# Chunk 0's own convolution taps in a bank of their own, and chunk 7's diagonals built earlier

## The chip, the cores and the metric

One NeuronCore of one Trainium2 chip runs the whole program. The metric is the device time of one execution in microseconds (us), the median of the runs.

## The reference, cut to what matters

The program computes two transformer-like layers (a pooling mixer, sliding-window attention, two gated feed-forward blocks), and after them a block with a Conformer convolution and an MLP, all in float32 for 512 tokens of width 1024. The change lies within the Conformer convolution:

```python
def conformer_conv(x, w_in, b_in, conv_w, conv_b, ln_g, ln_b, w_out, b_out):
    a, g = jnp.split(x @ w_in + b_in, 2, axis=-1)
    h = a * jax.nn.sigmoid(g)
    h = lax.conv_general_dilated(          # depthwise, 31 taps, padded in front
        h, conv_w[:, None, :].astype(h.dtype), window_strides=(1,),
        padding=[(CONV_KERNEL - 1, 0)],
        dimension_numbers=("NWC", "WIO", "NWC"),
        feature_group_count=D_MODEL) + conv_b
    h = jax.nn.silu(layer_norm(h, ln_g, ln_b))
    return h @ w_out + b_out
```

Each of the 1024 channels is convolved with 31 taps of its own: the output at token t is the sum over k of w[k] times h[t - 30 + k], plus a bias.

## The kernel before, in words

Activations lie transposed: 128 channels on the partitions and 512 tokens along them, so the 1024 channels are 8 chunks (C = 8). Five engines work side by side: TensorE (PE), VectorE (DVE), ScalarE (ACT), GpSimd (POOL) and SyncE (SP, which issues DMAs). Each runs its own list of instructions in order and waits for the others by semaphores.

**Projections.** A weight unit is 128 columns of a weight matrix. SP loads it into one of four slots of `raw` (L460), ACT makes the rounded high part `whi` (L988), and the low part `wlo` = raw - whi is made by DVE (`split_lo`, L1349), or, for the fourteen units of `OTHER_LOW` (6 to 19), by POOL (L602) or by an adding DMA that POOL issues (L596) after ACT has negated the high part (L1270). A chain is 8 tiles of three matmuls each (L628 to L630), 24 in all, into one of the banks 0 to 3. Units 0 to 15 of the stage `ain` are the gate and the value halves of the 8 chunks in turn: chains 2c and 2c+1 belong to chunk c.

**The convolution of chunk c.** DVE evicts the gate half (`evict(c, 0)`, L1750) to `tmp`, ACT takes its sigmoid (L1283), DVE evicts the value half to `taps`, which is bank 5 (`evict(c, 1)`, L1750), and forms hc (L1760) from `taps` and the sigmoid. The 31 taps of hc are then shared out:

- PE takes `PE_TAPS[c]` of them as matmuls with diagonal matrices (`convolve`, L906). For these, SP issues `SHIFTS[c]` DMAs (`shift_hc`, L496) that copy hc into `shifted` at several offsets, and DVE builds the diagonals `dg` in one instruction (`diagonals`, L1728). They sum in bank 6 or 7 (by c mod 2).
- ACT multiplies `POOL_TAPS[c]` of them (L1261) into a ring of nine buffers `tapped`, and POOL adds these up in `prod` (L614). ACT waits for POOL to give back a buffer of the ring.
- DVE takes the rest: its own taps (`own_tap`, L1704 for the first and L1707 for the others), done before PE's matmuls on the same bank, and `LATE_TAPS[c]` late ones (L1717), done after them and during the next chunk. Chunk 0 has 12 own taps and 2 late ones, chunk 1 seven and 8, chunk 6 three and none, chunk 7 eleven and none.

At the end `collect(c)` (L1744) adds bank 6 or 7 and `prod` into `hv`. ACT squares `hv` (L1278), and PE sums both over the channels (`statistics`, L920).

**Which comes first in a bank.** For the chunks 0 to 6 DVE's first own tap writes bank 6 or 7 and PE's diagonal matmuls add to it, so `convolve(c)` waits until all own taps are done (L902). Chunk 7 (`APART`) is treated otherwise: its own taps go to `taps` and the last of them to `hv`, PE's first round opens the bank with `start`, and `collect` first adds `prod` and `hv` (L1739) and then the bank. Ahead of the stage, in `first_chains`, PE writes banks 6 and 7 once with a matmul each (L656).

**The order of the work.** PE (L924 to L935): in the round of chunk c the two chains of chunk c, `convolve(c - 1)`, `statistics(c - 3)`. Chunk 0's two chains are interleaved, with the feature sums of the norm (L672) ahead of their last tiles; DVE makes the norm's `rinv` from these (L1771 to L1776) before the first eviction. DVE (L1764 to L1803): in the round of c, `gated(c)` (value eviction and hc), `diagonals(c)`, then the own taps of c mixed with the late taps of c - 1 and, between them, the low parts of later units (L1792) and the gate eviction of chunk c + 1 (L1794), and last `collect(c - 1)`. In the round of chunk 6, `diagonals(7)` and `gated(7)` come after all taps. POOL (L606 to L620): for each chunk its sums, with low parts made or added after the sums that `LOW_AT` names. SP (`load_conv_stage`, L498): the loads of the units in turn, with `shift_hc(c)` after the load of unit 2c + 6.

Of the kernel before, what the change touches and what calls it, by code (L numbers as in the profile page):

```python
# [28 lines left out]
P = 128  # L29
D = 1024  # L30
T = 512
C = D // P
# [9 lines left out]
TAPS = 31  # L42
PE_TAPS = (6, 6, 8, 8, 12, 12, 20, 14)
SHIFTS = (2, 2, 4, 4, 4, 4, 4, 2)
APART = C - 1
GROUP = tuple(P // s for s in SHIFTS)
ROUNDS = tuple(n // s for n, s in zip(PE_TAPS, SHIFTS))
SPREAD = {s: (SHIFTS.index(s), C - SHIFTS[::-1].index(s)) for s in set(SHIFTS)}
PAIR_TAPS = {s: max(n for n, e in zip(PE_TAPS, SHIFTS) if e == s) - s + 1 for s in SPREAD}
QUADRANT = P // 4  # L50
GATE_AT = 8
DIAGS = 2
POOL_TAPS = (11, 10, 10, 9, 9, 9, 8, 6)
LATE_TAPS = (2, 8, 10, 12, 9, 7, 0, 0)
# [117 lines left out]
def build(nc, xT, vec_in, cst_in, w_in, out):  # L172
# [3 lines left out]
    with ExitStack() as ctx:  # L176
# [68 lines left out]
        taps = bank[5]  # L245
# [94 lines left out]
        def own_taps(c):  # L340
            return range(PE_TAPS[c] + POOL_TAPS[c], TAPS - LATE_TAPS[c])
# [283 lines left out]
        def _(pe):  # L625
# [17 lines left out]
            def first_chains(name, norm_name, n=2):  # L643

                p = ph[name]
                wait_low(pe, p.unit + n - 1)
                pe.wait_ge(acc_free, p.chain + n - 4)
                for t in range(C):
                    if t == C - 2 and norm_name != "ffn0":
                        sum_features(norm_name)  # L650
                        if norm_name == "ain":
                            sum_features(norm_name, 1)
                    pe.wait_ge(xl_ready, X[norm_name] + t + 1 + (C if norm_name == "ffn1" else 0))
                    if name == "ain" and t == 0:
                        for b in range(2):
                            nc.tensor.matmul(bank[6 + b][:], whi[:, 0, 0:P], xh[:, 0, :], start=True, stop=True)  # L656
                    w = slice(t * P, (t + 1) * P)
                    for k in range(n):
                        mm = three(acc[k][:], whi[:, k, w], wlo[:, k, w], xh[:, t, :], xl[:, t, :],
                                   t == 0, t == C - 1)  # L660
                        if t == C - 1:
                            mm.then_inc(chain_done, 1)
                if norm_name == "ffn0":
                    sum_features(norm_name)
# [230 lines left out]
            def convolve(c):  # L895
                b, group = c % 2, GROUP[c]
                pe.wait_ge(hc_shifted[b], 16 * sum(SHIFTS[b:c + 1:2]))
                pe.wait_ge(diag_ready, c + 1)
                if c >= 2:
                    pe.wait_ge(hv_ready, c - 1)  # L900
                if c != APART:
                    pe.wait_ge(tap_steps, sum(len(own_taps(e)) for e in range(c + 1)))  # L902
                for q in range(ROUNDS[c]):
                    for g in range(SHIFTS[c]):
                        rows, at = slice(g * group, (g + 1) * group), SHIFTS[c] * q
                        mm = nc.tensor.matmul(bank[6 + b][rows, :], dg[:, c % DIAGS, q, rows],  # L906
                                              shifted[:, b, g, at:at + T],
                                              start=(q == 0 and c == APART), stop=(q == ROUNDS[c] - 1),
                                              skip_group_check=True)
                mm.then_inc(conv_done, 1)  # L910

# [428 lines left out]
        def _(dve):  # L1340
# [356 lines left out]
            def own_tap(c, n, k):  # L1697

                x, w = hc[:, c % HC, k:k + T], v("conv_w", c * TAPS + k)
                at = taps[:] if c == APART else bank[6 + c % 2][:]  # L1700
                if n == 0:
                    if 2 <= c != APART:
                        dve.wait_ge(hv_ready, c - 1)
                    V.tensor_scalar(at, x, w, None, ALU.mult).then_inc(tap_steps, 1)  # L1704
                    return
                dve.wait_ge(tap_steps, sum(len(own_taps(j)) for j in range(c)) + n)
                V.scalar_tensor_tensor(hv[:, c, :] if c == APART and n == len(own_taps(c)) - 1 else at, x, w, at,  # L1707
                                       op0=ALU.mult, op1=ALU.add).then_inc(tap_steps, 1)

            def late_tap(c, n, k):  # L1710
# [8 lines left out]
            def diagonals(c):  # L1719

                if c >= DIAGS:
                    dve.wait_ge(conv_done, c - DIAGS + 1)
                if c == 0:
                    dve.wait_ge(pairs_loaded, 16 * sum(s * s + 1 for s in SPREAD))
                shifts, rounds, group = SHIFTS[c], ROUNDS[c], GROUP[c]
                shape = [P, rounds, shifts, group]
                w = pair_w[shifts][:, :, c - SPREAD[shifts][0], 0:shifts * (rounds - 1) + 1:shifts]
                V.tensor_tensor(dg[:, c % DIAGS, 0:rounds].rearrange("p q (g n) -> p q g n", g=shifts),  # L1728
                                pair_id[shifts][:].rearrange("p (q g n) -> p q g n", q=1, g=1).broadcast_to(shape),
                                w.rearrange("p g (q n) -> p q g n", n=1).broadcast_to(shape), ALU.mult)\  # L1730
                    .then_inc(diag_ready, 1)

            def collect(c):

                part = prod[:, c % 2, :]
                dve.wait_ge(tapped_steps, sum(POOL_TAPS[:c + 1]) - c - 1)
                if c == APART:
                    dve.wait_ge(tap_steps, sum(len(own_taps(j)) for j in range(c + 1)))
                    V.tensor_tensor(hv[:, c, :], part, hv[:, c, :], ALU.add).then_inc(own_added, 1)  # L1739
                    part = hv[:, c, :]  # L1740
                    dve.wait_ge(own_added, 1)
                dve.wait_ge(late_steps, sum(LATE_TAPS[:c + 1]))
                dve.wait_ge(conv_done, c + 1)
                V.tensor_tensor(hv[:, c, :], bank[6 + c % 2][:], part, ALU.add).then_inc(hv_ready, 1)  # L1744

            def evict(c, j):

                k = 2 * (c % 2) + j
                dve.wait_ge(chain_done, p.chain + 2 * c + j + 1)
                V.tensor_tensor(taps[:] if j else tmp[:, k, :], acc[k][:], rinv[:], ALU.mult).then_inc(acc_free, 1)  # L1750

            def gated(c):
# [11 lines left out]
            for c in range(C):  # L1764
# [24 lines left out]
                for n in range(rounds):  # L1789
                    for j in range(2):  # L1790
                        if n == split_at[j] and c < C - 1 and (c or j) and 2 * c + j + AHEAD not in OTHER_LOW:
                            split_lo(p.unit, 0, 2 * c + j + AHEAD)  # L1792
                    if n == gate_at and c < C - 1:
                        evict(c + 1, 0)  # L1794
                    if n < len(own):
                        own_tap(c, n, own[n])
                    if 0 <= n - LATE_START[c] < len(late):
                        late_tap(c - 1, n - LATE_START[c], late[n - LATE_START[c]])
                if c == C - 2:
                    diagonals(C - 1)  # L1800
                    gated(C - 1)
                if c:
                    collect(c - 1)  # L1803
# [127 lines left out]
```

## Time and profile before

| | us |
|---|---|
| median of 3 runs | 1448.79 |
| lowest, highest run | 1448.34, 1451.68 |
| the profiled execution | 1449.69 |
| its span | 1447.9 |
| PE busy in the span | 1429.1 |
| DVE busy | 918.1 |
| ACT busy | 614.2 |
| POOL busy | 226.6 |

The profiled execution is one more run than the three, with the profiler on; its span is the time from the first to the last instruction on the core, and 1.8 us lie around it. The convolution stage takes some 130 of the 1447.9 us, from about 912 to 1042 us. Timelines and waits are read in us from the start of the span; a timeline row gives the start, the duration and, in brackets, how long the engine stood idle before it and what released it. Rows of like instructions in a run are merged (x12). The end of a PE matmul in it is modelled: successive ones overlap.

### The profile page before, as it was taken

The page shows a single profiled execution, that of the slowest core. Times are in us where ns is not written, and L with a number is a line of the kernel's source. Part 1 is how long each engine was busy: PE and PEld are TensorE (multiplying, and loading weights), DVE is VectorE, ACT ScalarE, POOL GpSimd, SP SyncE. Part 2 cuts the span into 40 slices and gives each one's busy share as a digit, 9 for nine tenths or more (in the row PEclk, how much of TensorE's full clock was granted, in tenths as well). Part 3 has the DMA queues.
Part 4 walks back from the last instruction along what each step waited for, and adds up shares of the span by engine and source line. Part 5 has one row for each costly group of instructions (what it writes and reads, how often), then busy time and mean ns, then how long its engine had stood idle before and what let it go on. Part 6 is the DMA issues. An engine that isn't in the chain of part 4 may idle for free.

```text
span 1447.9 us, 19992 instructions
## 1 busy us (share of the span) xinstructions
PE 1429.1 (99%) x6886; PEld 1168.4 (81%) x6886; DVE 918.1 (63%) x1320; ACT 614.2 (42%) x914; POOL 226.6 (16%) x172
## 2 busy tenths in 40 slices
PE   8999999999999999999999999899999999999999
PEld 7788888888887898888888888666588888888887
DVE  7877773573655667767754756889888653544532
ACT  5544442342546665444432424668554322222210
POOL 7100000000302231000000004599711000000000
PEclk9999999999999999999999999999999999999999
DMA  5233233232431012332332332249713332332321
GB/s 191 88 101 102 88 101 116 73 101 91 122 102 59 30 60 88 101 102 87 102 116 73 101 98 91 88 112 227 194 53 102 116 103 88 100 102 88 101 95 51
DMA packets 49756, 144.95 MB, mean 100 GB/s; under 512 B 10016, under 2 KB 10784, under 8 KB 49696
## 3 DMA queue, kind: packets, MB, share of 16 engines
q1 hardware_dynamic: 47408, 137.34, 30.0%
q0 software_dynamic: 1440, 5.24, 2.0%
q10 hardware_dynamic: 848, 1.59, 0.3%
q8 instruction: 35, 0.57, 0.2%
q14 instruction: 25, 0.20, 0.0%
HBM read 135.14 MB, written 2.10 MB: 95 GB/s over the span
## 4 chain that ended last, share of the span: by engine, by line
PE 91%; POOL 4%; issue 2%; DMA 1%; DVE 1%; ACT 1%; SPq 0%; ACTq 0%; POOLq 0%; DVEq 0%
PE bank L628 29%; PE bank L630 28%; PE bank L629 28%; POOL prod L614 2%; PE bank L779 1%; PE bank L807 1%; POOL res L563 1%; PE bank L792 1%; DMA shifted<-hc 1%; DMA res<-xT 1%; POOL ssum L573 1%; PE bank L906 1%; PE bank L966 0%; PE bank L965 0%; PE bank L672 0%
## 5 line engine op out<-in xcount | busy, mean ns | idle before, releaser
L628 PE MATMUL bank<-xh,whi 128*128 128x512 f32 x1184 | 465.4, 393 | 0.2
L630 PE MATMUL bank<-xh,wlo 128*128 128x512 f32 x1184 | 461.4, 390 | 0.0
L629 PE MATMUL bank<-xl,whi 128*128 128x512 f32 x1184 | 461.3, 390 | 0.0
L988 ACT ACTIVATE whi<-raw 128x1024 fp32r<-128x1024 f32 x244 | 255.6, 1050 | 242.0 <-PE bank L630 237.7
L1349 DVE TENSOR_TENSOR wlo<-raw,whi 128x1024 fp32r<-128x1024 f32 x230 | 287.9, 1252 | 42.8 <-ACT whi L988 34.7
L628 PEld LDWEIGHTS bank<-xh,whi 128*128 128x128 f32 x1184 | 222.4, 188 | 53.7 <-issue 5.2
L630 PEld LDWEIGHTS bank<-xh,wlo 128*128 128x128 f32 x1184 | 222.4, 188 | 46.6
L629 PEld LDWEIGHTS bank<-xl,whi 128*128 128x128 f32 x1184 | 222.5, 188 | 46.1 <-issue 1.0
L630 PE MATMUL bank<-ahi,wlo 128*128 128x512 f32 x608 | 236.8, 389 | 0.0
L628 PE MATMUL bank<-ahi,whi 128*128 128x512 f32 x608 | 236.8, 389 | 0.0
L629 PE MATMUL bank<-alo,whi 128*128 128x512 f32 x608 | 236.8, 389 | 0.0
L1370 DVE TENSOR_TENSOR res<-bank,res 128x512 f32 (+1 forms) x80 | 55.2, 690 | 199.9 <-PE bank L630 199.9
L573 POOL TENSOR_TENSOR ssum<-ssum,sq 128x512 f32<-128x512 f32 x32 | 49.2, 1538 | 721.0 <-ACT sq L1008 388.5
L1424 DVE SCALAR_TENSOR_TENSOR tmp<-u,vec,tmp 128x512 f32<-128x512 f32 x176 | 124.0, 747 | 29.5 <-ACT tmp L1050 29.5
L629 PEld LDWEIGHTS bank<-alo,whi 128*128 128x128 f32 x608 | 114.2, 188 | 23.8
L630 PEld LDWEIGHTS bank<-ahi,wlo 128*128 128x128 f32 x608 | 114.2, 188 | 23.5
L628 PEld LDWEIGHTS bank<-ahi,whi 128*128 128x128 f32 x608 | 114.2, 188 | 23.5
L1050 ACT ACTIVATE tmp<-u,vec 128x512 f32<-128x512 f32 x88 | 71.4, 814 | 121.6 <-DVE u L1417 121.5
L1417 DVE TENSOR_TENSOR u<-bank,rinv 128x512 f32<-128x512 f32 x88 | 59.5, 686 | 64.1 <-PE bank L630 64.1
L614 POOL TENSOR_TENSOR prod<-prod,tapped 128x512 f32<-128x512 f32 x56 | 77.8, 1390 | 6.8 <-ACT tapped L1261 0.4
L1072 ACT ACTIVATE ahi<-tmp 128x512 f32 (+1 forms) x32 | 20.2, 632 | 121.9 <-DVE tmp L1450 121.9
L1054 ACT ACTIVATE gate<-tmp 128x512 f32<-128x512 f32 x44 | 27.9, 633 | 98.4 <-DVE tmp L1424 98.4
(191 smaller groups left out, 1312.0 us busy)
## 6 DMA issues: line engine op xcount, KB each, us to landing
raw<-w_ffn_up SPq DMA_DIRECT2D x88, 512.0 KB, 3.4
raw<-w_ffn_down SPq DMA_DIRECT2D x32, 512.0 KB, 3.3
raw<-w_mlp_up SPq DMA_DIRECT2D x32, 512.0 KB, 3.3
raw<-w_mlp_down SPq DMA_DIRECT2D x32, 512.0 KB, 3.3
raw<-w_ain SPq DMA_DIRECT2D x16, 512.0 KB, 3.6
raw<-w_ffn_down SPq DMA_DIRECT2D x16, 384.0 KB, 3.0
raw<-w_qkv SPq DMA_DIRECT2D x12, 512.0 KB, 3.5
raw<-w_wo SPq DMA_DIRECT2D x8, 512.0 KB, 3.3
```

The costliest lines, as they stand in the source:

```text
L573: nc.gpsimd.tensor_tensor(ssum[:, which, :], ssum[:, which, :], x, ALU.add)\
L614: nc.gpsimd.tensor_tensor(prod[:, c % 2, :], a, tapped[:, (made + k) % PARTS, :], ALU.add)\
L628: nc.tensor.matmul(out_, hi, mh, start=first, stop=False)
L629: nc.tensor.matmul(out_, hi, ml, start=False, stop=False)
L630: return nc.tensor.matmul(out_, lo, mh, start=False, stop=last)
L988: nc.scalar.activation(whi[:, s, 0:tiles * P], raw[:, s, 0:tiles * P], ACT.Copy)\
L1050: nc.scalar.activation(tmp[:, k, :], u[:, k, 2:2 + T], ACT.Identity, scale=col(vec, par + 2), bias=col(vec, par + 3))\
L1054: nc.scalar.activation(gate[:, b, :], tmp[:, 2 * b + 1, :], ACT.Silu)\
L1349: V.tensor_tensor(wlo[:, s, 0:tiles * P], raw[:, s, 0:tiles * P], whi[:, s, 0:tiles * P].bitcast(F32), ALU.subtract).then_inc(lo_done, 1)
L1370: V.tensor_tensor(row(res, c), acc[k][:], row(res, c), ALU.add).then_inc(acc_free, 1)
L1417: V.tensor_tensor(u[:, k, 2:2 + T], acc[k][:], rinv[:], ALU.mult).then_inc(acc_free, 1)
L1424: V.scalar_tensor_tensor(tmp[:, k, :], u[:, k, shift:shift + T], col(vec, par + 4 * j + shift), tmp[:, k, :], op0=ALU.mult, op1=ALU.add).t ...
```

## The change

`APART` becomes a tuple with chunk 0 beside chunk 7. So chunk 0's twelve own taps are summed in `taps` and its last one goes to `hv`; `convolve(0)` no longer waits for them and opens bank 6 itself with `start`; the matmul that wrote bank 6 ahead of the stage goes; `collect(0)` has the added operation L1739 with a wait behind it; and the value eviction of chunk 1, which writes `taps` anew, waits for chunk 0's own taps. The second part moves `diagonals(7)`: from behind all taps in the round of chunk 6 to the step n = 5 of that round's loop (`LAST_DIAGONALS = 5`), where it stands behind `evict(7, 0)` and ahead of the last two late taps of chunk 5.

```diff
--- before.py
+++ after.py
@@ -42,13 +42,14 @@
 TAPS = 31
 PE_TAPS = (6, 6, 8, 8, 12, 12, 20, 14)
 SHIFTS = (2, 2, 4, 4, 4, 4, 4, 2)
-APART = C - 1
+APART = (0, C - 1)
 GROUP = tuple(P // s for s in SHIFTS)
 ROUNDS = tuple(n // s for n, s in zip(PE_TAPS, SHIFTS))
 SPREAD = {s: (SHIFTS.index(s), C - SHIFTS[::-1].index(s)) for s in set(SHIFTS)}
 PAIR_TAPS = {s: max(n for n, e in zip(PE_TAPS, SHIFTS) if e == s) - s + 1 for s in SPREAD}
 QUADRANT = P // 4
 GATE_AT = 8
+LAST_DIAGONALS = 5
 DIAGS = 2
 POOL_TAPS = (11, 10, 10, 9, 9, 9, 8, 6)
 LATE_TAPS = (2, 8, 10, 12, 9, 7, 0, 0)
@@ -652,8 +653,7 @@
                             sum_features(norm_name, 1)
                     pe.wait_ge(xl_ready, X[norm_name] + t + 1 + (C if norm_name == "ffn1" else 0))
                     if name == "ain" and t == 0:
-                        for b in range(2):
-                            nc.tensor.matmul(bank[6 + b][:], whi[:, 0, 0:P], xh[:, 0, :], start=True, stop=True)
+                        nc.tensor.matmul(bank[7][:], whi[:, 0, 0:P], xh[:, 0, :], start=True, stop=True)
                     w = slice(t * P, (t + 1) * P)
                     for k in range(n):
                         mm = three(acc[k][:], whi[:, k, w], wlo[:, k, w], xh[:, t, :], xl[:, t, :],
@@ -898,14 +898,14 @@
                 pe.wait_ge(diag_ready, c + 1)
                 if c >= 2:
                     pe.wait_ge(hv_ready, c - 1)
-                if c != APART:
+                if c not in APART:
                     pe.wait_ge(tap_steps, sum(len(own_taps(e)) for e in range(c + 1)))
                 for q in range(ROUNDS[c]):
                     for g in range(SHIFTS[c]):
                         rows, at = slice(g * group, (g + 1) * group), SHIFTS[c] * q
                         mm = nc.tensor.matmul(bank[6 + b][rows, :], dg[:, c % DIAGS, q, rows],
                                               shifted[:, b, g, at:at + T],
-                                              start=(q == 0 and c == APART), stop=(q == ROUNDS[c] - 1),
+                                              start=(q == 0 and c in APART), stop=(q == ROUNDS[c] - 1),
                                               skip_group_check=True)
                 mm.then_inc(conv_done, 1)
 
@@ -1697,14 +1697,14 @@
             def own_tap(c, n, k):
 
                 x, w = hc[:, c % HC, k:k + T], v("conv_w", c * TAPS + k)
-                at = taps[:] if c == APART else bank[6 + c % 2][:]
+                at = taps[:] if c in APART else bank[6 + c % 2][:]
                 if n == 0:
-                    if 2 <= c != APART:
+                    if c >= 2 and c not in APART:
                         dve.wait_ge(hv_ready, c - 1)
                     V.tensor_scalar(at, x, w, None, ALU.mult).then_inc(tap_steps, 1)
                     return
                 dve.wait_ge(tap_steps, sum(len(own_taps(j)) for j in range(c)) + n)
-                V.scalar_tensor_tensor(hv[:, c, :] if c == APART and n == len(own_taps(c)) - 1 else at, x, w, at,
+                V.scalar_tensor_tensor(hv[:, c, :] if c in APART and n == len(own_taps(c)) - 1 else at, x, w, at,
                                        op0=ALU.mult, op1=ALU.add).then_inc(tap_steps, 1)
 
             def late_tap(c, n, k):
@@ -1734,11 +1734,11 @@
 
                 part = prod[:, c % 2, :]
                 dve.wait_ge(tapped_steps, sum(POOL_TAPS[:c + 1]) - c - 1)
-                if c == APART:
+                if c in APART:
                     dve.wait_ge(tap_steps, sum(len(own_taps(j)) for j in range(c + 1)))
                     V.tensor_tensor(hv[:, c, :], part, hv[:, c, :], ALU.add).then_inc(own_added, 1)
                     part = hv[:, c, :]
-                    dve.wait_ge(own_added, 1)
+                    dve.wait_ge(own_added, APART.index(c) + 1)
                 dve.wait_ge(late_steps, sum(LATE_TAPS[:c + 1]))
                 dve.wait_ge(conv_done, c + 1)
                 V.tensor_tensor(hv[:, c, :], bank[6 + c % 2][:], part, ALU.add).then_inc(hv_ready, 1)
@@ -1747,6 +1747,8 @@
 
                 k = 2 * (c % 2) + j
                 dve.wait_ge(chain_done, p.chain + 2 * c + j + 1)
+                if j and c - 1 in APART:
+                    dve.wait_ge(tap_steps, sum(len(own_taps(e)) for e in range(c)))
                 V.tensor_tensor(taps[:] if j else tmp[:, k, :], acc[k][:], rinv[:], ALU.mult).then_inc(acc_free, 1)
 
             def gated(c):
@@ -1792,12 +1794,13 @@
                             split_lo(p.unit, 0, 2 * c + j + AHEAD)
                     if n == gate_at and c < C - 1:
                         evict(c + 1, 0)
+                    if n == LAST_DIAGONALS and c == C - 2:
+                        diagonals(C - 1)
                     if n < len(own):
                         own_tap(c, n, own[n])
                     if 0 <= n - LATE_START[c] < len(late):
                         late_tap(c - 1, n - LATE_START[c], late[n - LATE_START[c]])
                 if c == C - 2:
-                    diagonals(C - 1)
                     gated(C - 1)
                 if c:
                     collect(c - 1)
```

## Rows read from the trace of the kernel before

**Rows 1.** The page, part 1: busy us (share of the span) xinstructions.

```profile
PE 1429.1 (99%) x6886; PEld 1168.4 (81%) x6886; DVE 918.1 (63%) x1320; ACT 614.2 (42%) x914; POOL 226.6 (16%) x172
```

**Rows 2.** The list of waits, 905 to 1060 us: in total, times, longest.

```profile
PE bank L906 <- DVE bank L1707: 5.9, 1, 5.9
```

**Rows 3.** Timeline of PE: start us, us, engine, line, form, count, idle before.

```profile
911.36 0.62 PE L656 MATMUL bank<-xh,whi 128*128 128x512 f32 x2
...
935.10 0.39 PE L630 MATMUL bank<-xh,wlo 128*128 128x512 f32 x1
941.43 4.14 PE L906 MATMUL bank<-shifted,dg 128*64 128x512 f32 x12 [5.94 <-DVE bank L1707]
...
956.62 2.79 PE L906 MATMUL bank<-shifted,dg 128*64 128x512 f32 x12
...
983.55 0.39 PE L630 MATMUL bank<-xh,wlo 128*128 128x512 f32 x1
985.99 1.92 PE L906 MATMUL bank<-shifted,dg 128*32 128x512 f32 x16 [2.06 <-DMA shifted<-hc]
```

**Rows 4.** Stretches: length, busy us (xinstructions) by engine, PEclk, DMA share.

```profile
941.40:945.50 4.10, 4.07 (x12) 1.24 (x12) 3.96 (x4) 2.72 (x5) 4.10 (x3) 0.66 0.33 68
...
986.00:1028.00 42.00, 42.00 (x236) 29.50 (x240) 37.33 (x50) 29.28 (x42) 39.42 (x32) 1.00 0.98 233
```

**Rows 5.** Timeline of SP's queue, the shift copies of chunks 0 and 3.

```profile
929.88 1.27 SPq L496 DMA_DIRECT2D shifted<-hc  x2
...
973.57 4.28 SPq L496 DMA_DIRECT2D shifted<-hc  x4
```

**Rows 6.** Timeline of DVE, lines of the convolution stage.

```profile
921.89 0.69 DVE L1771 TENSOR_SCALAR rinv<-bank 128x512 f32<-128x512 f32 x1 [3.01 <-PE bank L672]
...
934.19 1.22 DVE L1349 TENSOR_TENSOR wlo<-raw,whi 128x1024 fp32r<-128x1024 f32 x1
...
938.16 3.12 DVE L1707 SCALAR_TENSOR_TENSOR bank<-hc,vec,bank 128x512 f32<-128x512 f32 x4
...
945.50 1.65 DVE L1349 TENSOR_TENSOR wlo<-raw,whi 128x1024 fp32r<-128x1024 f32 x1
...
953.19 0.69 DVE L1744 TENSOR_TENSOR hv<-bank,prod 128x512 f32<-128x512 f32 x1
956.72 0.70 DVE L1750 TENSOR_TENSOR bank<-bank,rinv 128x512 f32<-128x512 f32 x1 [2.85 <-PE bank L630]
...
972.79 0.75 DVE L1760 SCALAR_TENSOR_TENSOR hc<-bank,vec,gate 128x512 f32<-128x512 f32 x1 [1.52 <-ACT gate L1283]
...
1024.60 1.08 DVE L1728 TENSOR_TENSOR dg<-pair_id,pair_w 128x896 f32<-128x896 f32 x1
1027.98 0.70 DVE L1750 TENSOR_TENSOR bank<-bank,rinv 128x512 f32<-128x512 f32 x1 [2.29 <-PE bank L630]
...
1039.53 0.69 DVE L1739 TENSOR_TENSOR hv<-prod,hv 128x512 f32<-128x512 f32 x1
```

**Rows 7.** Timeline of ACT, end of chunk 2 and the sigmoid of chunk 3.

```profile
970.47 0.72 ACT L1261 ACTIVATE tapped<-hc,vec 128x512 f32<-128x512 f32 x1 [0.53 <-POOL prod L614]
...
972.05 0.71 ACT L1283 ACTIVATE gate<-tmp,vec 128x512 f32<-128x512 f32 x1
```

**Rows 8.** Timeline of POOL.

```profile
931.42 1.29 POOL L614 TENSOR_TENSOR prod<-tapped 128x512 f32<-128x512 f32 x1 [13.62 <-ACT tapped L1261]
...
953.31 5.58 POOL L614 TENSOR_TENSOR prod<-prod,tapped 128x512 f32<-128x512 f32 x4
...
969.14 1.29 POOL L614 TENSOR_TENSOR prod<-tapped 128x512 f32<-128x512 f32 x1
```

**Rows 9.** DMA issues, 929 to 936 us: count, size, median us to landing.

```profile
shifted<-hc SPq DMA_DIRECT2D x2, 258.0 KB, 3.5
```

**Rows 10.** Chain of waits, 928 to 945 us: start us, us, what.

```profile
934.30 2.25 POOL prod L614
...
936.68 1.28 POOL prod L614
```

## The prediction

> **What bounds the kernel now.** I read the page first: TensorE (PE) is busy for 99% of the span, so only its few idle places can be won [rows 1]. The list of waits inside the convolution stage names the largest of them: PE stood still for 5.9 us before chunk 0's diagonal matmuls (L906), released by VectorE's (DVE's) last own tap (L1707) [rows 2]. PE's timeline places it: its last chain matmul ends at 935.49 (935.10 + 0.39), L906 starts at 941.43 [rows 3]. That is the wait the change takes away. The question is whether the end of the stage hears of it, so I followed what comes next. PE stops again at 983.94 (983.55 + 0.39) and starts chunk 3's diagonal matmuls at 985.99, released by the DMA of chunk 3's shifted copies [rows 3]. From 986 to 1028 it is busy 42.00 of 42.00 us [rows 4]. So in this stage, what is done before 985.99 counts only as far as it brings that landing forward.
>
> What sets that landing? Going back: the four shift DMAs are issued from 973.57 [rows 5], right after hc of chunk 3 (L1760 at 972.79), for which DVE had been idle 1.52 us waiting for ScalarE's (ACT's) sigmoid [rows 6]. ACT's sigmoid at 972.05 stands in its queue behind the last product of chunk 2 at 970.47, and that one waited for GpSimd's (POOL's) sum L614 to give back a buffer of the ring [rows 7]. POOL's first sum of chunk 2 starts at 969.14 [rows 8]; POOL has no gap worth the name from 931.42 to that point (four sums take 5.58 us, 1.28 each with 0.15 between them). POOL is therefore the bound of this stretch: 931.42 (first sum) to 970.4, then ACT, hc, DMA, PE at 985.99. None of it waits for PE, nor for the own taps of chunk 0.
>
> **Part A, chunk 0's own taps in the bank apart.**
>
> 1. The wait of 5.94 us before L906 goes. The shift DMAs of chunk 0 are issued at 929.88 [rows 5] and land some 3.5 us after issue [rows 9], so around 934; PE can start at 935.49 and no longer at 941.43.
>
> 2. Late next is the low part of the fifth weight unit, L1349 on DVE. Before the change, two chains (48 matmuls) fill the 11.05 us between the end of L906 at 945.57 (941.43 + 4.14) and 956.62, so 5.5 us each [rows 3]. Afterwards: L906 from 935.49 to 938.3, chain 4 to 943.8, but L1349 for chain 5 ends only at 947.15 (945.50 + 1.65) [rows 6], and nothing in the edit moves it, as DVE does the same taps at the same times in another bank. So 3.3 us of the wait come back here. Chain 5 ends at 952.7; chunk 1's diagonals still wait for its own taps, done at about 953.2 [rows 6]. They start there instead of at 956.62: 3.4 us of the 5.94 are left.
>
> 3. Those 3.4 us end at chunk 3. PE is free at about 980.5 and the landing is where it was. The wait of 2.06 us [rows 3] becomes 5.5 us. Gain at the end of the stage: 0. Chunk 2's copies are also sent earlier, because DVE's idle 2.85 us before L1750 at 956.72 go and that eviction, and hc of chunk 2 behind it, come some 2 us sooner [rows 6]; whatever wait is left there drowns in the wait at chunk 3.
>
> 4. One of two matmuls of L656 is dropped. Both take 0.62 us together and one 0.39 [rows 3], so the second costs 0.23. PE works back to back there until the feature sums, and DVE idles 3.01 us for these [rows 6]; all that follows, POOL's stream too, starts 0.23 us sooner: **-0.23**.
>
> 5. Merging costs one more DVE operation, L1739: 0.69 us where chunk 7 has it [rows 6], and a wait behind it of some 0.1 us. On DVE it is covered: it goes in at 953.19, where DVE has 2.85 us idle ahead of 956.72 [rows 6]. Queued behind it are L1744, chunk 2's eviction and hc; by the sum 953.19 + 0.69 + 0.1 + 0.69 the eviction starts at 954.7, still 2 us sooner than now. Without cover it would cost 0.8.
>
> 6. But POOL pays for it. L1739 has both inputs in SBUF, and the rows show what such an operation does to POOL: at 934.19 DVE starts L1349 (1.22 us, two SBUF inputs) [rows 6] and POOL's sum at 934.30 takes 2.25 us, the next one 1.28 [rows 10], so 0.97 for 1.22. Taps and evictions, with one input in PSUM, leave POOL at 1.28. L1739 runs from 953.19 to 953.88, and POOL's next sum would start at 953.31 [rows 8]. Between nothing (if it fell wholly beside POOL's own gap) and 1.28 (if a lost turn displaced a whole sum) I take the distance to DVE's end, 0.57; scaling 0.97/1.22 to 0.69 gives 0.55. POOL is the bound up to 985.99, so it goes into the end: **+0.57**. The Trainium skill (SBUF — State Buffer, section Who interferes with whom) says the same against this change: a DVE instruction with two SBUF inputs and a GpSimd instruction reading SBUF exclude each other for the whole instruction. By its word alone the term would be the full 0.69 at most, a sum 0.12 us higher.
>
> 7. The longer idle has a price of its own. After the idle 5.94 us chunk 0's twelve matmuls took 4.14 us; chunk 1's twelve, of the same form and without idle, 2.79 [rows 3]. The granted clock was 0.66 in the first stretch and 1.00 from 986 on, after 2.06 us idle [rows 4]: part of that first stretch ran at 1.2 GHz in place of 2.4. Today this costs nothing, since the wait at chunk 3 takes it up. With the change the long idle (5.5, plus 0.57 of item 6, about 6.1 us) stands directly ahead of 42 us without slack. 6.1 is nearest to 5.94, so I take the same price, 4.14 - 2.79: **+1.35**. Bounds: 0, as after 2.06 us, and about 2.
>
> 8. The new wait for tap_steps ahead of chunk 1's eviction L1750: the taps end at 941.28 (938.16 + 3.12) [rows 6], the eviction starts about 0.1 us later than now. Behind it stand hc of chunk 1, and so ACT's products and SP's shift DMAs. POOL has chunk 0's products and a weight part to do until then: 0.
>
> **Part B, chunk 7's diagonals earlier.** One DVE instruction, L1728 at 1024.60, of 1.08 us [rows 6], moves ahead of chunk 5's last two late taps and behind chunk 7's first eviction, which ACT's sigmoid waits for, so the sigmoid is not touched. It issues no DMA and passes nothing on SP or POOL. Its wait for chunk 5's matmuls was met long before. The late taps go back by 1.08, and before L1750 at 1027.98 DVE is idle 2.29 us either way, waiting for PE's chain [rows 6]: 0. With no cover it would cost 1.08; meeting a POOL sum of 1.28 it takes 2.36 at worst, 0.07 over the cover. Nor can it gain: nobody waits for these diagonals.
>
> **Sum.** -0.23 + 0.57 + 1.35 = +1.69 us. The profiled execution took 1449.69 us (span 1447.9), 0.90 above the median of the three runs, 1448.79; it would go to 1451.4, the median to **1450.5**. A measurement of this kernel can tell about 0.3%, that is 4.35 us, from no change, so this counts as the same.
>
> **Rivals.**
>
> *The clock doesn't fall before chunk 3* (chance 0.37). The idle there is as long as the one that did it, which speaks against; for it, there is a single such case in the trace. Then the sum is +0.34: 1449.1.
>
> *The gain is kept* (0.05). If something other than POOL's stream placed the landing ahead of 985.99, so that it moved with PE, the 5.94 us of idle and the 1.35 of slow clock would be won: -5.94 - 1.35 - 0.23 + 0.57 = -6.95, 1441.8. Against it: L1349 at 945.50 alone takes back 3.3, and the chain from hc of chunk 3 to POOL has no link to PE [rows 6, 7].
>
> *Slower* (0.04). PE stays at 1.2 GHz through chunk 3's matmuls and the whole of chain 10: another 5.5 us of matmuls at twice their time, +7.2 in all, 1456.0. It decides once PE runs some 5.4 us longer at the low clock than it does after the idle today (half of that is the missing 2.7 to 4.35). For it: the work right behind has no slack at all. Against: today the clock is back within the twelve matmuls and the next chain runs at full pace.
>
> *The change doesn't free PE* (0.02). If chunk 0's copies landed late, as the slowest kind would, L906 would start near 940. The end would be that of the second case, 1449.1.
>
> The forecast itself has 0.52. **Range**: the low end is the second case without the POOL term (1448.6) less 0.45, by which the fastest run lies below the median, and 0.3 for overlaps of POOL and DVE that fall better: 1447.8. The high end is 1450.5 with 0.7 for POOL (1.28 instead of 0.57), 0.4 for the clock, and 1.0 for the runs, one of which lay 2.89 above the median: 1452.6. Faster by over 0.3%: 0.05, the kept gain. Slower: 0.04. Within: 0.91.
>
> **What would show it.** Right: L906's first matmuls start near 935.3 with no wait; PE idles some 3 us ahead of the fifth chain for L1349; chunk 1's diagonals come near 953; and the wait for shifted ahead of chunk 3's is 5 to 6.5 us, with a granted clock under 1.00 after it. POOL's sum at 953 takes about 1.8 us, and L1760 of chunk 3 stands at 973.1 or so. Wrong: L1760 of chunk 3 comes before 972, PE starts chunk 3's diagonals before 985, or DVE's idle before chunk 7's second eviction is gone.

## The result, and the profile after

The changed kernel is **slower by 0.19%**: the ratio to the kernel before, run beside it, is 1.0019 with a 95% interval from 1.0011 to 1.0027, which on 1449.7 us is +2.75 us (1.6 to 3.9). The median of its 20 runs is 1453.13 us (1448.31 to 1458.11), that of 20 runs of the kernel before 1449.74 (1448.34 to 1454.17). The runs of the changed kernel lie 9.8 us apart, those of the kernel before 5.8.

The page of the changed kernel's profile, parts 1 and 5 (columns as in [rows 1]; L629 is the former L628, as the lines moved by one):

```profile
PE 1432.6 (99%) x6885; PEld 1170.8 (81%) x6885; DVE 919.7 (63%) x1321; ACT 614.2 (42%) x914; POOL 226.0 (16%) x172
...
L629 PE MATMUL bank<-xh,whi 128*128 128x512 f32 x1184 | 465.6, 393 | 3.5 <-DVE wlo L1349 3.4
```

PE is busy 3.5 us more, with one matmul fewer. A longer busy time for less work points at the clock. The list of waits (905 to 1060 us) names what took the place of the 5.9 us of [rows 2]. (The three waits of its first row are those of chunks 3, 5 and 7, of 4.60, 1.26 and some 1.6 us; the kernel before had 2.06 at chunk 3 and 1.66 at chunk 7.)

```profile
PE bank L906 <- DMA shifted<-hc: 7.5, 3, 4.6
...
PE bank L629 <- DVE wlo L1349: 3.4, 1, 3.4
```

Timeline of PE in the same stage, to be laid beside [rows 3]:

```profile
934.29 2.79 PE L906 MATMUL bank<-shifted,dg 128*64 128x512 f32 x12
...
946.21 0.79 PE L629 MATMUL bank<-xh,whi 128*128 128x512 f32 x1 [3.44 <-DVE wlo L1349]
953.45 2.80 PE L906 MATMUL bank<-shifted,dg 128*64 128x512 f32 x12
...
967.29 1.92 PE L906 MATMUL bank<-shifted,dg 128*32 128x512 f32 x16
985.37 3.64 PE L906 MATMUL bank<-shifted,dg 128*32 128x512 f32 x16 [4.60 <-DMA shifted<-hc]
1001.26 2.78 PE L906 MATMUL bank<-shifted,dg 128*32 128x512 f32 x24
1016.83 2.78 PE L906 MATMUL bank<-shifted,dg 128*32 128x512 f32 x24 [1.26 <-DMA shifted<-hc]
```

Chunk 0's matmuls (first row) start with no wait. Then 3.44 us come back ahead of the fifth chain (counted from 0, as in the prediction: the value half of chunk 2), and chunk 3's matmuls wait 4.60 us instead of 2.06 and take 3.64 us instead of 1.92 for the same sixteen. Last, chunk 5's wait 1.26 us where before they waited for nothing. The stretches around it give the clock (PEclk is the third figure from the end):

```profile
946.20:953.40 7.20, 7.20 (x24) 5.62 (x24) 7.09 (x11) 2.80 (x5) 7.06 (x5) 0.76 0.42 146
...
980.80:985.30 4.50, 0.00 (x0) 0.00 (x0) 4.09 (x6) 2.98 (x5) 4.21 (x4) 0.83 1.02 266
985.30:992.00 6.70, 6.63 (x32) 2.85 (x33) 5.58 (x7) 6.49 (x10) 6.27 (x6) 0.61 1.00 264
992.00:1001.00 9.00, 9.00 (x42) 7.38 (x40) 7.31 (x11) 5.47 (x8) 8.43 (x8) 1.00 1.01 238
```

A granted clock between 0.5 and 1.00 is a stretch that ran in part at 1.2 and in part at 2.4 GHz. The clock fell twice to 1.2 GHz: behind the 3.44 us of idle (the fifth chain, 24 matmuls, then took 7.2 us, not 5.5), and within the 4.60 us, staying low for most of the 6.7 us after it (0.61). In [rows 4] the stretch from 986 on ran at 1.00.

DVE and POOL show that the stream which sets the landing has hardly moved (timeline of DVE, then of POOL, then of SP's queue):

```profile
952.19 0.69 DVE L1739 TENSOR_TENSOR hv<-prod,hv 128x512 f32<-128x512 f32 x1
952.92 0.69 DVE L1744 TENSOR_TENSOR hv<-bank,hv 128x512 f32<-128x512 f32 x1
...
954.50 0.75 DVE L1762 SCALAR_TENSOR_TENSOR hc<-bank,vec,gate 128x512 f32<-128x512 f32 x1 [0.24 <-ACT gate L1283]
...
972.02 0.75 DVE L1762 SCALAR_TENSOR_TENSOR hc<-bank,vec,gate 128x512 f32<-128x512 f32 x1 [2.27 <-ACT gate L1283]
...
1026.35 2.22 DVE L1728 TENSOR_TENSOR dg<-pair_id,pair_w 128x896 f32<-128x896 f32 x1
...
1031.18 0.70 DVE L1752 TENSOR_TENSOR bank<-bank,rinv 128x512 f32<-128x512 f32 x1 [1.15 <-PE bank L631]
```

```profile
952.29 6.03 POOL L615 TENSOR_TENSOR prod<-prod,tapped 128x512 f32<-128x512 f32 x4
...
968.37 1.29 POOL L615 TENSOR_TENSOR prod<-tapped 128x512 f32<-128x512 f32 x1
...
1002.73 0.86 POOL L597 DMA_DIRECT2D wlo<-w_ain  x1
```

```profile
972.79 4.24 SPq L497 DMA_DIRECT2D shifted<-hc  x4
...
1002.94 5.97 SPq L497 DMA_DIRECT2D shifted<-hc  x4
```

**Where the 3.3 us between the two spans are (1451.2 against 1447.9).** This execution reached the stage 0.90 us sooner, ahead of anything that was changed (L656 at 910.46, before at 911.36), and 0.23 us come from the dropped matmul. From POOL's first sum on (930.29, before 931.42) its first sum of chunk 2 comes 38.08 us later, before 37.72: +0.36. Chunk 3's matmuls start +0.51 late against that same origin, chunk 4's +3.00 (1001.26 against 999.39, and 1.13 sooner at the origin), chunk 5's +4.33 (1016.83 against 1013.63). After that nothing is added. So: -0.90 - 0.23 + 0.51 + 2.49 (low clock) + 1.33 (chunk 5's wait) = +3.20. The first term has nothing to do with the change, so between these two executions the change is worth +4.1 us, more than the +2.75 of the ratio.

### The profile page after: what moved, and what is told of

It reads as the page before. It is cut to its first block, busy times and chain, and to the rows that moved or that the text cites. A ratio compares the mean times of both kernels' runs of the same rounds, so it can differ in the third digit from the quotient of the medians.

```text
span 1451.2 us, 19993 instructions
## 1 busy us (share of the span) xinstructions
PE 1432.6 (99%) x6885; PEld 1170.8 (81%) x6885; DVE 919.7 (63%) x1321; ACT 614.2 (42%) x914; POOL 226.0 (16%) x172
## 3 DMA queue, kind: packets, MB, share of 16 engines
q0 software_dynamic: 1440, 5.24, 2.0%
## 4 chain that ended last, share of the span: by engine, by line
PE 92%; POOL 2%; DMA 2%; issue 1%; DVE 1%; ACT 1%; SPq 0%; ACTq 0%; POOLq 0%; DVEq 0%
PE bank L629 29%; PE bank L630 28%; PE bank L631 28%; POOL prod L615 2%; DMA shifted<-hc 1%; PE bank L721 1%; PE bank L779 1%; PE bank L807 1%; PE bank L792 1%; PE bank L746 1%; PE bank L906 0%; SPq L497 0%; PE bank L965 0%; PE bank L966 0%; PE bank L672 0%
## 5 line engine op out<-in xcount | busy, mean ns | idle before, releaser
L629 PE MATMUL bank<-xh,whi 128*128 128x512 f32 x1184 | 465.6, 393 | 3.5 <-DVE wlo L1349 3.4
L1349 DVE TENSOR_TENSOR wlo<-raw,whi 128x1024 fp32r<-128x1024 f32 x230 | 288.7, 1255 | 41.8 <-ACT whi L988 33.6
L629 PEld LDWEIGHTS bank<-xh,whi 128*128 128x128 f32 x1184 | 222.7, 188 | 56.8 <-issue 5.6
L629 PE MATMUL bank<-ahi,whi 128*128 128x512 f32 x608 | 236.5, 389 | 0.0
L629 PEld LDWEIGHTS bank<-ahi,whi 128*128 128x128 f32 x608 | 114.1, 188 | 23.6
```

The source lines that it names most:

```text
L629: nc.tensor.matmul(out_, hi, mh, start=first, stop=False)
L1349: V.tensor_tensor(wlo[:, s, 0:tiles * P], raw[:, s, 0:tiles * P], whi[:, s, 0:tiles * P].bitcast(F32), ALU.subtract).then_inc(lo_done, 1)
```

## The experiments

All in five rounds with the kernel before beside them. Differences in us are the ratio times 1449.6.

**Which part.** First the two parts apart. Part A alone, against the changed kernel:

```diff
-                    if n == LAST_DIAGONALS and c == C - 2:
-                        diagonals(C - 1)
...
                 if c == C - 2:
+                    diagonals(C - 1)
                     gated(C - 1)
```

> Part A alone; chunk 7's diagonals stay where they were. Theory (the loss of 2.7 us comes from the long idle and low clock ahead of chunk 3's diagonal matmuls, and what follows from it): the same +2.7 us over the kernel before, 1.5 to 4 by the scatter, with a wait of 4.5 to 6 us for shifted ahead of chunk 3. Rival (part B costs: its instruction took 2.22 us in the changed kernel where it had 1.08): 1 us or more less than that, about +1.5.

Measured: ratio 1.0034 (1.0022 to 1.0046), +4.9 us, only six runs. Its profile shows 3.97 us of idle ahead of chunk 3 and sixteen matmuls in 3.40 us. The loss is there without part B. The point lies higher than for the whole change, but the two intervals overlap, and I read nothing into it.

Part B alone, against the kernel before:

```diff
                         evict(c + 1, 0)
+                    if n == 5 and c == C - 2:
+                        diagonals(C - 1)
...
                 if c == C - 2:
-                    diagonals(C - 1)
                     gated(C - 1)
```

> Part B alone: chunk 7's diagonals behind the gate eviction, everything else as before. Theory: 0 within 0.5 us, since DVE waits for PE's chain ahead of chunk 7's second eviction either way. Rival (part B costs): +0.5 to +1.2 us, and DVE's idle before that eviction gone.

Measured: 1.0002 (0.9993 to 1.0010), +0.3 us: nothing. DVE's timeline:

```profile
1022.27 1.28 DVE L1728 TENSOR_TENSOR dg<-pair_id,pair_w 128x896 f32<-128x896 f32 x1
...
1027.10 0.70 DVE L1750 TENSOR_TENSOR bank<-bank,rinv 128x512 f32<-128x512 f32 x1 [2.08 <-PE bank L630]
```

The instruction has moved, and DVE still idles 2.08 us for PE. In the changed kernel it took 2.22 us and the idle is 1.15, still above zero.

**Is it the moved idle?** The changed kernel with one wait back:

```diff
-                if c not in APART:
+                if c != C - 1:
                     pe.wait_ge(tap_steps, sum(len(own_taps(e)) for e in range(c + 1)))
```

> The changed kernel, but chunk 0's diagonal matmuls wait for chunk 0's own taps again, as before the change; bank apart, merging operation and part B stay. Theory: the idle is back at 941 us where nothing pays for it, the one ahead of chunk 3 is 2.1 to 2.8 us and the clock does not fall there: the time returns to that of the kernel before, +0.1 to +0.4 us (POOL's stretch 0.36 less the dropped matmul 0.23). Rival (the merging operation L1739 and its wait cost, not the moved idle): still +2.5 us or so.

Measured: 1.0004 (0.9995 to 1.0013), +0.6 us. PE's timeline:

```profile
941.51 4.97 PE L906 MATMUL bank<-shifted,dg 128*64 128x512 f32 x12 [5.94 <-DVE hv L1707]
...
986.11 1.93 PE L906 MATMUL bank<-shifted,dg 128*32 128x512 f32 x16 [1.25 <-DMA shifted<-hc]
```

The bank apart, the merging operation and the dropped matmul are all in it, and the loss of the median is gone; what went in is a wait of 5.94 us. So the rival (merging is the loss) falls, though by the interval (-0.7 to +1.9 us) it may have a small share, and the place of the idle is what matters. The low clock is here too, in chunk 0's matmuls (4.97 us), where nobody is kept by it.

**Is it the clock?** PE was to be kept at work in the idle ahead of chunk 3, with matmuls of ones into bank 3, which is free there:

```diff
+                if c == 4:
+                    pe.wait_ge(acc_free, p.chain + 8)
+                    for _ in range(36):
+                        nc.tensor.matmul(acc[3][:, 0:P], ones[:], ones[:], start=True, stop=True)
                 if c >= 1:
                     convolve(c - 1)
```

> The changed kernel with 36 small matmuls of ones (some 0.11 us each, 4.0 us) in the idle ahead of chunk 3's diagonal matmuls, into a bank that is free. Theory: PE doesn't stand idle there, the clock stays at 2.4 GHz after it, chunk 3's sixteen matmuls take 1.9 us again and not 3.6, chunk 5's copies come as early as before, and the time goes down by 2.5 us, to +0.2 us over the kernel before. Rival (the clock is a symptom, the landing and DVE set the end): the time stays at +2.7 us although the clock is 1.00.

Measured: 1.0023 (1.0013 to 1.0033), +3.3 us: a miss. Each filling matmul is two in the trace, so they took 8.20 us and held chunk 3's back to 990.79, 61.85 us behind chunk 0's hc and not 57.39 as in the changed kernel. The clock was 1.00 behind them, but this run can't tell what that is worth. The same with half of them:

```diff
-                    for _ in range(36):
+                    for _ in range(18):
```

> As the run with 36 filling matmuls, but 18, since each turned out to be two of 0.11 us: some 4.1 us in an idle of 4 to 5, so that they end ahead of the landing. Theory (the low clock behind the idle is what costs most): chunk 3's sixteen matmuls take 1.9 us, chunk 5 no longer waits for its copies, time down to 0 to +0.7 us over the kernel before. Rival (the landing and POOL's adding DMAs cost whatever the clock does): still +2 us or more, with the 1.1 to 1.3 us wait for shifted ahead of chunk 5.

Measured: 0.9996 (0.9987 to 1.0005), -0.6 us. PE's timeline and the stretch behind:

```profile
980.51 4.18 PE L932 MATMUL bank<-ones 128*128 128x128 f32 x36
984.92 1.93 PE L906 MATMUL bank<-shifted,dg 128*32 128x512 f32 x16 [0.23 <-DMA shifted<-hc]
```

```profile
984.90:992.00 7.10, 7.08 (x45) 4.66 (x46) 6.65 (x9) 5.36 (x8) 6.67 (x6) 1.00 0.99 270
```

The idle would be as long as in the changed kernel (4.4 us, against 4.60), only it is filled; hc of chunk 3 comes 44.02 us behind chunk 0's, as in the changed kernel (44.04), and the matmuls start 56.89 us behind it, 0.5 sooner; the sixteen matmuls take 1.93 us. With that the whole loss is gone, chunk 5's wait too (no wait in its row), and the runs lie within 3.0 us (1448.38 to 1451.35) where those of the changed kernel spread over 9.8. The low clock behind the idle is what costs, with what it draws after it: nothing but the filling differs between the two kernels.

**Is it the merging operation on POOL?** The sum into bank 6 first, so that no operation of the merge has two SBUF inputs:

```diff
-                if c in APART:
+                if c == 0:
...
+                    V.tensor_tensor(bank[6][:], bank[6][:], part, ALU.add).then_inc(own_added, 1)
+                    part = hv[:, 0, :]
+                    dve.wait_ge(own_added, 1)
+                elif c in APART:
```

> The changed kernel, but chunk 0's prod is added into bank 6 and then the bank to hv, so that no merging operation has two inputs in SBUF. Theory (L1739 holds up POOL's sum): POOL's four sums from 952 to 958 take 5.6 us and not 6.0, chunk 3's copies land 0.4 us sooner; the time only 0.4 us below that of the changed kernel, +2.3 us, hardly to be told apart. Rival (the merging operation is the main cost): back to +0.3 us or less.

Measured: 1.0024 (1.0014 to 1.0034), +3.5 us. POOL's timeline:

```profile
953.25 5.59 POOL L615 TENSOR_TENSOR prod<-prod,tapped 128x512 f32<-128x512 f32 x4
```

Four sums in 5.59 us, as in [rows 8], against 6.03: the merge does cost POOL 0.44 us, and it is not the loss. In this execution the clock fell at chunk 3 (sixteen matmuls in 3.64 us) and once more at chunk 5 (PE's timeline):

```profile
1017.81 4.20 PE L906 MATMUL bank<-shifted,dg 128*32 128x512 f32 x24 [2.57 <-DMA shifted<-hc]
```

The same 24 matmuls take 2.78 us at full pace (the row at 1016.83 of the changed kernel). So chunk 5's wait can cost twice, by itself and by the clock behind it.

**What sets the landing?** Two of chunk 1's taps go from ACT and POOL to DVE (the same computation, summed in another order):

```diff
-POOL_TAPS = (11, 10, 10, 9, 9, 9, 8, 6)
-LATE_TAPS = (2, 8, 10, 12, 9, 7, 0, 0)
+POOL_TAPS = (11, 8, 10, 9, 9, 9, 8, 6)
+LATE_TAPS = (2, 10, 10, 12, 9, 7, 0, 0)
```

> The changed kernel with two of chunk 1's taps taken from ACT and POOL (10 to 8) and given to DVE's late taps (8 to 10), which fall where DVE stood idle 3.5 us. Theory (POOL's stream sets the landing of chunk 3's copies): two sums of 1.4 us fewer, hc of chunk 3 2 to 2.8 us sooner, PE's idle ahead of chunk 3 some 2 us, no low clock there: -1.5 to -2.5 us against the kernel before, 4 to 5 below the changed kernel. Rival (DMA contention sets the landing, not POOL): unchanged, +2.7 us.

Measured on the changed kernel: 0.9986 (0.9976 to 0.9995), -2.0 us. PE's timeline:

```profile
954.23 2.79 PE L906 MATMUL bank<-shifted,dg 128*64 128x512 f32 x12
...
982.10 1.93 PE L906 MATMUL bank<-shifted,dg 128*32 128x512 f32 x16 [0.55 <-DMA shifted<-hc]
```

Chunk 0's hc was at 927.51 there and chunk 3's at 968.97, 41.46 us apart, against 44.04 in the changed kernel: 2.6 us sooner for two sums fewer. The edit takes two products from ACT too, but ACT had been waiting for POOL there ([rows 7]), so POOL's stream did set the landing. DVE no longer idles ahead of chunk 3's hc, so it is now the bound, with POOL close behind it. The same edit in the kernel before:

> The same two taps moved in the kernel before, without the change. Theory: PE's 2.1 us of idle ahead of chunk 3 bound the gain, and DVE has less room there: -1 to -1.8 us, so less than with the change, whose gain then shows. Rival (the change has nothing to give even with POOL out of the way): the same time as with the change, or less.

Measured: 1.0027 (1.0017 to 1.0036), +3.9 us, where a gain was expected. DVE's timeline has chunk 3's hc at 973.33 with no idle before it, 44.38 us behind chunk 0's (before: 43.68): DVE, which waits for PE until 957.12 in that kernel, takes the two taps behind it and becomes the bound at once. Its diagonals of chunk 2 took 2.65 us there besides, 0.77 in the run before this one. And the copies meet POOL's adding DMAs, which now go out sooner (PE's timeline, then SP's queue):

```profile
986.64 1.92 PE L906 MATMUL bank<-shifted,dg 128*32 128x512 f32 x16 [2.31 <-DMA shifted<-hc]
1001.41 2.78 PE L906 MATMUL bank<-shifted,dg 128*32 128x512 f32 x24 [1.31 <-DMA shifted<-hc]
```

```profile
974.10 5.93 SPq L496 DMA_DIRECT2D shifted<-hc  x4
987.63 6.89 SPq L496 DMA_DIRECT2D shifted<-hc  x4
```

So the change does have its worth once the resource behind it is relieved: about 5.9 us lie between these two kernels, of which 2.0 are a gain over the kernel before and 3.9 a loss that the moved taps bring without the change. PE's lead becomes room on DVE: chunk 2's eviction comes 26.82 us behind chunk 0's hc with the change and 28.17 without. That is 1.35 of the 2.92 us by which chunk 3's hc comes sooner; the 1.88 us of the diagonals cover the rest. The profiled execution of the second kernel took 1451.74 us, less than its median of 1453.08, so its trace doesn't show the whole 3.9.

**The collision at chunk 5.** In the changed kernel POOL's adding DMA (1002.73) goes out 0.2 us ahead of chunk 5's copies (1002.94), and SP needs 5.97 us for the four. Two adding DMAs one sum later:

```diff
-LOW_AT = {... 14: (4, 5), 15: (4, 7), 16: (5, 6), ...
+LOW_AT = {... 14: (4, 6), 15: (4, 7), 16: (5, 7), ...
```

> The changed kernel with two of POOL's adding DMAs put one sum later (unit 14 behind chunk 4's sixth sum, unit 16 behind chunk 5's seventh), so that they no longer go out within 0.3 us of the shift copies of chunks 5 and 6. Theory (part of the loss is this collision, 1.1 to 1.3 us at chunk 5; the low clock ahead of it stays): SP's four copies of chunk 5 are issued in 4.3 us and not 6.0, no wait for shifted ahead of chunk 5, +1.3 to +2 us over the kernel before, so 1 us under the changed kernel. Rival (the late start of chunk 5's copies alone makes the wait): the wait of 1.1 us or more stays, +2.7 us.

Measured: 1.0021 (1.0010 to 1.0032), +3.0 us, not under the changed kernel. In its profiled execution (1450.40 us, among its fastest) the four were issued in 4.25 us and chunk 5 waited for nothing:

```profile
984.82 3.58 PE L906 MATMUL bank<-shifted,dg 128*32 128x512 f32 x16 [4.21 <-DMA shifted<-hc]
...
1001.65 4.25 SPq L497 DMA_DIRECT2D shifted<-hc  x4
```

As far as the wait goes, the traces tell the theory and its rival apart. In the changed kernel chunk 4's matmuls and chunk 5's hc both come 3.00 us late against POOL's first sum, so the late start alone leaves no wait; what is added is the time to issue the copies, which took 4.45 us in the kernel before:

```profile
1001.07 4.45 SPq L496 DMA_DIRECT2D shifted<-hc  x4
```

With the adds later, chunk 5's hc stands 0.90 us behind the start of chunk 4's matmuls, as in the changed kernel (1002.16 and 1001.26), the issue took 4.25 us, and there is no wait. With 36 fillings the copies started later still (1005.86), were issued in 4.32 us, and again no wait. Of all the profiled executions chunk 5's matmuls waited in the four whose issue took 5.7 us or more (by 1.11 to 2.66 us) and in no other. So the wait goes with the slow issue and not with the late start. But the median doesn't follow: the other runs with the adds later reach 1456.3, the low clock at chunk 3 is still there (3.58 us), and what share the wait has in the median stays open.

**A version that beats both.** In the run with two taps moved, the fifth chain still ran slow (clock 0.64 from 945.7 to 954.2), and DVE, now the bound, waited 1.20 us for it. Filling that idle:

```diff
                 for k in (2 * (c % 2), 2 * (c % 2) + 1) if c else ():
+                    if c == 2 and k == 1:
+                        pe.wait_ge(acc_free, p.chain + 4)
+                        for _ in range(13):
+                            nc.tensor.matmul(acc[3][:, 0:P], ones[:], ones[:], start=True, stop=True)
```

> The changed kernel with two of chunk 1's taps moved from POOL to DVE, and 13 filling matmuls (0.23 us each, 3.0 us) in the 3.4 us idle ahead of the fifth chain. Theory (with POOL out of the way DVE's run from chunk 2's eviction on sets the landing, so the low clock in the fifth chain now costs): that eviction comes 0.8 to 1.1 us sooner after chunk 0's hc, chunk 3's hc too, and the time is 0.5 to 1.1 us under the run without the filling, -2.5 to -3.2 us against the kernel before. Rival (the low clock there is hidden as in the changed kernel): the same -2.0 us.

Measured: 1.0007 (0.9992 to 1.0021), +1.0 us, against the expectation. PE's timeline:

```profile
943.20 3.06 PE L931 MATMUL bank<-ones 128*128 128x128 f32 x26
946.79 0.50 PE L629 MATMUL bank<-xh,whi 128*128 128x512 f32 x1 [0.53 <-DVE wlo L1353]
...
983.06 3.42 PE L906 MATMUL bank<-shifted,dg 128*32 128x512 f32 x16 [2.73 <-DMA shifted<-hc]
...
1014.92 2.78 PE L906 MATMUL bank<-shifted,dg 128*32 128x512 f32 x24 [2.66 <-DMA shifted<-hc]
```

It is the change's own story once more: PE got faster ahead of chunk 3 and chunk 2's eviction came 1.28 us sooner, but DVE then waited 1.72 us for ACT's sigmoid, so chunk 3's hc hardly came sooner (41.34 us behind chunk 0's, 41.46 before). The idle of PE there grew from 0.55 to 2.73 us, the clock fell, and chunk 5 waited 2.66 us. Nine filling matmuls at chunk 3 besides:

```diff
+                if c == 4:
+                    pe.wait_ge(acc_free, p.chain + 8)
+                    for _ in range(9):
+                        nc.tensor.matmul(acc[3][:, 0:P], ones[:], ones[:], start=True, stop=True)
```

> The run before (two taps of chunk 1 from POOL to DVE, 13 fillings ahead of the fifth chain), with 9 more filling matmuls (2.05 us) in the 2.7 us of idle that it had ahead of chunk 3's diagonal matmuls. Theory (that run lost its gain because PE came earlier to chunk 3, stood idle longer, and the clock fell there): clock 1.00 behind chunk 3, sixteen matmuls in 1.9 us, no wait for shifted at chunk 5, -2.3 to -3 us against the kernel before, and less scatter than any run without filling. Rival (the fillings or the tap split cost for themselves): +0.5 us as in that run.

Measured: 0.9978 (0.9969 to 0.9987), **-3.2 us**, 1445.53 to 1448.76 in eleven runs: faster than the kernel before and some 6 us faster than the changed one. That it is faster than the run with two taps moved and nothing filled (-2.0, -3.5 to -0.7) is not shown, as the intervals overlap; its runs lie closer together (3.2 us against 7.0).

```profile
981.30 2.17 PE L936 MATMUL bank<-ones 128*128 128x128 f32 x18
984.06 1.93 PE L906 MATMUL bank<-shifted,dg 128*32 128x512 f32 x16 [0.59 <-DMA shifted<-hc]
```

```profile
985.30:992.00 6.70, 6.70 (x41) 4.97 (x34) 6.49 (x9) 6.67 (x10) 6.27 (x6) 1.00 0.98 244
```

## Why the prediction was right, and where it was off

The forecast was no change to speak of, with a sum of +1.69 us. It came out as +2.75 by the ratio, within the stated 0.3%. The mechanism was right up to chunk 3's matmuls; that the number fell inside owes something to the width of the range, for what was mis-sized and missed behind them (1.14 for the clock, 1.33 for chunk 5) is more in the profile than the whole forecast sum. By the ratio the time is 1451.5 on the median of the three runs, inside the range; the plain median of the twenty, 1453.13, lies 0.5 above its end.

- **Right: the wait of 5.94 us goes, 3.3 come back for L1349, the rest ends at chunk 3.** 3.44 us ahead of the fifth chain, and the landing 57.39 us behind chunk 0's hc against 56.88. POOL's sum beside L1739 took 1.74 us (forecast 1.8). The run with the wait put back shows that nothing of the 5.94 reached the end.
- **Right: what sets the landing.** Two sums fewer on POOL brought chunk 3's hc 2.6 us forward.
- **Right: part B costs nothing** (+0.3 us, interval across 0). That the instruction might take 2.36 us at worst was close: 2.22.
- **The dropped matmul, 0.23**: from the first L656 to POOL's first sum it is 19.83 us, before 20.06. No run tried it alone.
- **Item 6, POOL's stretch, was a little large**: 0.57 against 0.44 for the four sums and 0.36 by chunk 2. The row of a longer operation, scaled (0.55), was no nearer. The Trainium skill (SBUF — State Buffer, section Who interferes with whom) says that a DVE instruction with two SBUF inputs contends with a GpSimd instruction that reads SBUF. The trace agrees, with 0.44 us for an instruction of 0.69, and the run with one PSUM input in each operation of the merge took the stretch away.
- **Item 7, the clock, was the term that was mis-sized.** Forecast 1.35; in the profile 2.49. The step took the price from one case, a granted clock of 0.66 over 4.1 us; in the changed kernel it was 0.61 over 6.7 us. Even that one case was a draw: behind the same idle of 5.94 us chunk 0's twelve matmuls took 4.14 us in the kernel before, 4.70 with two taps moved in it, 4.97 with the wait back and 5.39 with part B alone, against 2.79 at full pace, so a price of 1.35 to 2.6. From the start of chunk 3's matmuls to that of chunk 4's it is 13.40 us in the kernel before, 15.09 in the run with part A alone, 15.16 with the adds later, 15.64 with the merge in the bank and 15.89 in the changed kernel: a price of 1.7 to 2.5 us at this place, behind idles of 3.97 to 4.61 us, that differs from run to run, where one row was taken for a constant. "About 2" as the upper bound was too low as well.
- **Missed: the clock falls at the fifth chain too.** The idle of 3.3 us was forecast there and given no price. Here it cost nothing, since chunk 3's idle took it up: 4.60 us, below the forecast 5 to 6.5. With two taps moved it kept DVE back by 1.28 us, and chunk 3's hc by 0.12.
- **Missed: chunk 5's wait, 1.33.** I had taken the 42 us behind chunk 3 as moving together. DVE waits for PE in it, and the copies move with both, but POOL's adding DMAs don't: before, one went out 2.58 us behind the start of chunk 5's copies, now 0.21 ahead of it, and the copies take longer to issue.

The rival in which the clock doesn't fall is what the kernel with the fitted filling shows: it was priced at +0.34 and measured -0.6 with an interval from -1.9 to +0.7. The rival with the gain kept fell. The scatter of the changed kernel, 1448.31 to 1458.11, goes in the main with the clock that each run was granted in the mean: the five runs at 0.998 have a median of 1451.2 us, the nine at 0.996 of 1452.2, the five at 0.995 of 1454.8, and the one at 0.994 took 1458.11. With the idle filled all eleven runs had 0.997 to 0.999. Two of the runs at 0.998 took 1453.4 and 1453.5 all the same, so the low clock is not all of the scatter, and where in the other runs it fell was not seen, for only one of them was profiled.

## What to carry to other kernels

Before taking a wait away, look for the next one of the same engine and ask what sets its end: if it doesn't move, the idle is only moved, and where it goes matters, since the slow clock behind a long idle can be free in one place and on the path in another. An idle that can't be removed can be filled with matmuls of no use, cut to the idle's length (with twice as many the whole loss was still there, +3.3 us). A price for the slow clock that was read once is one draw and not a constant. And a gain for one engine shows when the engine that comes next is relieved in the same step: the split of two taps was worth -2.0 us with the change and +3.9 without.

## What the runs showed of the hardware that was not expected

- Length of idle and fall of the clock don't go together strictly. Behind 2.73 us of idle ahead of chunk 3 the clock was 0.74 over the next 6.0 us, and behind 2.57 ahead of chunk 5 (merge in the bank) 0.76; behind 2.66 ahead of chunk 5, in the run with 13 fillings, it was 1.00. Behind 2.31 and 2.06 us PE's next sixteen matmuls took 1.92 us, the full pace. And 3.41 us of idle ahead of the fifth chain, in the run with the merge in the bank, left the clock at 1.00 over the next 6 us, where behind 3.44 in the changed kernel it was 0.76 over 7.2.
- SP's four issues of one chunk's copies took 4.1 to 4.5 us in most places, and 5.2 to 6.9 us wherever POOL's adding DMA went out within some 1.5 us of the first of them, before or after: 5.97 with 0.2 us between, 5.93 with 0.8, 6.89 with 0.05, 5.24 with 1.4. With POOL's 1.7 and 2.0 us ahead it was 4.94 and 4.77, with POOL's 2.6 us behind 4.24. The run with the adds later moved POOL's away and got 4.25; what holds SP up, no run tried.
- A 128x128 float32 matmul of ones appears as two matmuls of about 0.11 us each.
